# Turning x1 to rows by DMA instead of by TensorE, and an order for two early subtractions

## The reference

```
h  = RMSNorm(x, g_mix)
qa,ka,va,qb,kb,vb,ga,gb = split(h @ w_in)
ya = block-sparse causal attention, 8 heads;  yb = sliding-window attention, 8 query and 2 key heads
merged = sigmoid(ga + b) * (ya @ w_branch_a) + sigmoid(gb + b) * (yb @ w_branch_b)
x1  = x + merged @ w_out
out = x1 + square(relu(RMSNorm(x1, g_ffn) @ w_ff1)) @ w_ff2
```

## Time and profile before

| What | Value |
|---|---|
| median of 3 runs | 674.53 us (673.7 to 674.6) |
| the profiled execution's own time | 676.32 us |
| its span, first to last instruction | 674.5 us |
| TensorE busy | 667.3 us |
| VectorE busy | 504.3 us |
| ScalarE busy | 370.9 us |
| GpSimd busy | 323.7 us |
| transposes of x1 (32 matmuls, L1686) | 272 ns each |

### The profile page before, as it was taken

The page is one execution under the profiler, slowest core; times in us unless marked ns, Lnnn a source line. Parts: engine busy times, 40 slices in busy tenths (PEclk is TensorE's granted clock), DMA queues, the critical chain, the costliest instruction groups (busy, mean ns, idle before and its releaser), DMA issues.

```text
span 674.5 us, 9477 instructions
## 1 busy us (share of the span) xinstructions
PE 667.3 (99%) x3238; PEld 552.9 (82%) x3238; DVE 504.3 (75%) x701; ACT 370.9 (55%) x662; POOL 323.7 (48%) x197
## 2 busy tenths in 40 slices
PE   8999999999999999999999999999999999999997
PEld 7788888888888888888888888888888888888886
DVE  5767998655555555875559879787897888879797
ACT  6567676776666566534357546253553615546360
POOL 1246676466555662444445536246453444436432
PEclk9999999999999999999999999999999999999999
DMA  8322242223323113554222322315132151330303
GB/s 308 106 95 93 73 130 83 80 79 95 94 94 94 64 47 116 166 184 174 89 70 93 130 88 86 131 62 182 54 106 94 62 187 62 96 120 3 125 0 125
DMA packets 22909, 69.87 MB, mean 104 GB/s; under 512 B 2731, under 2 KB 4011, under 8 KB 22876
## 3 DMA queue, kind: packets, MB, share of 16 engines
q1 hardware_dynamic: 22588, 68.92, 30.8%
q10 hardware_dynamic: 288, 0.52, 0.2%
HBM read 67.27 MB, written 2.16 MB: 103 GB/s over the span
## 4 chain that ended last, share of the span: by engine, by line
PE 95%; DMA 1%; SPq 1%; ACT 1%; DVE 1%; issue 0%; DVEq 0%
PE bank L1396 21%; PE bank L1398 21%; PE bank L1397 21%; PE bank L1714 8%; PE bank L1716 8%; PE bank L1717 8%; PE bank L1563 3%; PE bank L1547 2%; PE bank L1584 1%; PE bank L1586 1%; DMA w_raw<-slabs 1%; SPq L449 1%; ACT store L665 1%; PE bank L1686 1%; PE bank L1424 0%; PE bank L1425 0%
## 5 line engine op out<-in xcount | busy, mean ns | idle before, releaser
L543 POOL TENSOR_TENSOR w_lo<-w_raw,w_hi 128x1024 fp32r<-128x1024 f32 x77 | 190.3, 2476 | 234.7 <-ACT w_hi L637 228.9
L1396 PE MATMUL bank<-qk_hi,w_hi 128*128 128x512 f32 x320 | 125.0, 391 | 0.0
L1398 PE MATMUL bank<-qk_hi,w_lo 128*128 128x512 f32 x320 | 124.5, 389 | 0.0
L1397 PE MATMUL bank<-qk_lo,w_hi 128*128 128x512 f32 x320 | 124.5, 389 | 0.0
L1396 PE MATMUL bank<-x_hi,w_hi 128*128 128x512 f32 x304 | 122.1, 402 | 0.0
L1398 PE MATMUL bank<-x_hi,w_lo 128*128 128x512 f32 x304 | 118.8, 391 | 0.0
L1397 PE MATMUL bank<-x_lo,w_hi 128*128 128x512 f32 x304 | 118.4, 389 | 0.0
L637 ACT ACTIVATE w_hi<-w_raw 128x1024 fp32r<-128x1024 f32 x80 | 83.9, 1057 | 55.9 <-PE bank L1398 52.7
L1279 DVE SCALAR_TENSOR_TENSOR store<-bank,softmax,store 128x512 f32<-128x512 f32 x101 | 71.9, 744 | 22.9 <-PE bank L1717 22.8
L1714 PE MATMUL bank<-v_parts,x_hi 128*128 128x512 f32 (+1 forms) x218 | 84.5, 387 | 0.3 <-issue 0.3
L1717 PE MATMUL bank<-v_parts,x_lo 128*128 128x512 f32 (+1 forms) x218 | 84.4, 387 | 0.0
(11 more groups left out here) (167 smaller groups left out, 1213.1 us busy)
## 6 DMA issues: line engine op xcount, KB each, us to landing
w_raw<-slabs SPq DMA_DIRECT2D x80, 512.0 KB, 3.3
bias_m<-slabs SPq DMA_DIRECT2D x16, 512.0 KB, 3.4
qk_hi_again<-slabs SPq DMA_DIRECT2D x16, 512.0 KB, 4.9
store<-x_t SPq DMA_DIRECT2D x16, 256.0 KB, 3.5
bias_m<-tab_dram SPq DMA_DIRECT2D x8, 256.0 KB, 4.2
out<-store SPq DMA_DIRECT2D x7, 256.0 KB, 2.5
bias_m<-tab_dram SPq DMA_DIRECT2D x8, 128.0 KB, 3.5
w_raw<-slabs ACTq DMA_DIRECT2D x2, 256.0 KB, 3.7
```

Source lines behind the costliest of these rows:

```text
L543: pool.tensor_tensor(w_lo[:, g % WS, :], w_raw[:, g % RAW, :], w_hi[:, g % WS, :].bitcast(F32), ALU.subtract).then_inc(w_lo_ready, 1)
L1396: pe.matmul(out_, wh, xh, start=first, stop=False)
L1397: pe.matmul(out_, wh, xl, start=False, stop=False)
L1398: last = pe.matmul(out_, wl, xh, start=False, stop=end)
```

## The change

The transposes of x1 leave TensorE. ScalarE copies tile n, as it stands in SBUF, into two planes of 16-bit numbers (the lower and the upper half of each float32), and issues one DMA that transposes both planes at once: 128x1024 16-bit numbers, 256 KB. GpSimd joins the turned halves into `x1_rows`, one tile after each of the low parts of slabs G_OUT+3 to G_FF+2. Planes and turned planes are rings of two. The final row copy on ScalarE in chunk 0 is gone, and its signal for the product buffers moves to the first part of the last w_out slab. At the start GpSimd waits for `x_sum_lo` before the low part of slab 4. The reserve of SBUF for DMA descriptors is smaller, which makes room for the planes.

```
-            def x1_rows_copy(n):            # ScalarE
-                act.wait_ge(x1t_done, n + 1)
-                act.activation(x1_rows[:, :, P * n:P * n + P], bank[n % 5]...,
-                               ACT.Copy).then_inc(x1_rows_ready, 1)
+            def x1_planes(n):
+                if n >= 2:
+                    act.wait_ge(planes_turned[n % 2], 16 * (n // 2))
+                of = store[:, n, :].bitcast(U16).rearrange("p (n h) -> p h n", h=2)
+                for h in range(2):
+                    act.activation(planes[n % 2][:, h, :], of[:, h, :], ACT.Copy).then_inc(planes_ready, 1)
+            def x1_turn(n):
+                act.wait_ge(planes_ready, 2 * n + 2)
+                if n >= 2:
+                    act.wait_ge(x1_rows_ready, n - 1)
+                act.dma_start_transpose(plane_rows[n % 2][...].rearrange("p h t n -> p (h t) n"),
+                                        planes[n % 2][...].rearrange("p h n -> p (h n)")).then_inc(
+                                            planes_turned[n % 2], 16)
             for n in range(N_OUT):
                 split_hi(G_OUT + n + 2)
                 act.wait_ge(acc_read, read(G_OUT + n))
                 act.activation(qk_hi[:, n, :], store[:, n, :], ...)
-                if n:
-                    x1_rows_copy(n - 1)
+                x1_planes(n)
+                x1_turn(n)
...
             square(0, 0)
-            x1_rows_copy(KT - 1)
             chunk(0, first=True)
```

```
             pool.wait_ge(w_lo_ready, 3)      # GpSimd
+            pool.wait_ge(xsum_lo_ready, 1)
             for s in range(4, G_GATE + 2):
...
+            def x1_rows_join(n):
+                pool.wait_ge(planes_turned[n % 2], 16 * (n // 2 + 1))
+                to = x1_rows[:, :, P * n:P * n + P].bitcast(U16).rearrange("p t (n h) -> p h t n", h=2)
+                for h in range(2):
+                    last = pool.tensor_copy(to[:, h, :, :], plane_rows[n % 2][:, h, :, :])
+                last.then_inc(x1_rows_ready, 1)
             for g in range(LATE + 2, G_FF + 3):
                 split_lo(g, g + 3)
+                if g >= G_OUT + 3:
+                    x1_rows_join(g - G_OUT - 3)
```

```
-            x1_transpose(0)                  # TensorE
             for n in range(2, N_OUT):
                 out_part(n, range(KT))
-                x1_transpose(n - 1)
...
             last.then_inc(slab_done, 1)      # the first w_ff1 slab
-            x1_transpose(N_OUT - 1)
```

More of the change, by code:

```diff
@@ L92, in build @@
 def build(nc, x_t, slabs, params, table, onehot, tab_dram, out):
-    F32, R = mybir.dt.float32, mybir.dt.float32r
+    F32, R, U16 = mybir.dt.float32, mybir.dt.float32r, mybir.dt.uint16
     ALU, ACT = mybir.AluOpType, mybir.ActivationFunctionType
@@ L136, in build @@
         par = sb("par", [P, N_PAR], F32)
+        planes = [sb(f"planes{i}", [P, 2, S], U16) for i in range(2)]
+        plane_rows = [sb(f"plane_rows{i}", [P, 2, QT, P], U16) for i in range(2)]
         softmax = sb("softmax", [P, 3, 8], F32)
@@ L250, in build @@
         x1_hi_ready, x1_lo_ready = sem("x1_hi_ready"), sem("x1_lo_ready")
-        x1t_done, x1_rows_ready = sem("x1t_done"), sem("x1_rows_ready")
+        planes_ready, x1_rows_ready = sem("planes_ready"), sem("x1_rows_ready")
+        planes_turned = [sem("planes_turned0"), sem("planes_turned1")]
         ms2_ready, r2_ready = sem("ms2_ready"), sem("r2_ready")
@@ L812, in _ @@
                 act.activation(x_hi[:, n, :], tmp_a, ACT.Copy).then_inc(m_hi_ready, 1)
-            def x1_rows_copy(n):
-                act.wait_ge(x1t_done, n + 1)
-                act.activation(x1_rows[:, :, P * n:P * n + P], bank[n % 5][:, :].rearrange("p (t n) -> p t n", t=QT),
-                               ACT.Copy).then_inc(x1_rows_ready, 1)
+            def x1_planes(n):
[8 more added lines that the diff above has]
+                    act.wait_ge(x1_rows_ready, n - 1)
+                act.dma_start_transpose(plane_rows[n % 2][:, :, :, :].rearrange("p h t n -> p (h t) n"),
+                                        planes[n % 2][:, :, :].rearrange("p h n -> p (h n)")).then_inc(
+                                            planes_turned[n % 2], 16)
             for n in range(N_OUT):
@@ L1676, in out_part @@
                     last = slab_part(g, bank[5 + n % 2], from_x, [kt], kt == 0, kt == KT - 1)
+                    if (n, kt) == (N_OUT - 1, 0):
+                        last.then_inc(product_done, 2 * PRODUCTS)
                 if kts[-1] == KT - 1:
                     last.then_inc(slab_done, 1)
[L1680 to L1689, removed]
             out_part(0, range(KT - 1))
@@ L1694, in _ @@
             out_part(1, range(2, KT))
-            x1_transpose(0)
             for n in range(2, N_OUT):
                 out_part(n, range(KT))
-                x1_transpose(n - 1)
             def up(j, c):
@@ L1833 @@
     arrays = {k: np.ascontiguousarray(v) for k, v in arrays.items()}
-    nc = bacc.Bacc("TRN2", target_bir_lowering=False, num_devices=1)
+    nc = bacc.Bacc("TRN2", target_bir_lowering=False, num_devices=1, dynamic_dma_scratch_size=2048)
     F32 = mybir.dt.float32
```

## The result

The changed kernel takes 675.75 us (median of 16 runs, 675.18 to 676.64), the kernel before 674.42 (16 runs beside it, 672.88 to 676.55): ratio 1.0018, 95% interval 1.0011 to 1.0026. That is 1.2 to 1.3 us slower, just inside the bound of 0.2%; the forecast was 672.5.

The account below looks back on a forecast made before the run. TensorE, busy 667.3 of 674.5 us, was taken as the bound. Transposes -3.8, early wait -1.5 and stall at up(3) +3.3 gave -2.0 us off the 674.53 median: 672.5, range 669.3 to 679.5.

Parts of the forecast that it names:

- the 3.8 us of the transposes: TensorE's w_out stage: removing 32 transposes, eight groups of 0.475 us each, takes 3.8 us off the path.
- what was called hidden: w_out stage: ScalarE's DMA issue (1.5 us), the DMA's landing (5) and seven of eight GpSimd joins cost nothing.
- C: ScalarE in the w_out stage: the transposing issue holds its queue over 2.6 us; at 4 us, 680.7; chance 0.14.
- D: DMA in the w_out stage: turns slower than slabs, at 8 us each +12, 686.5; chance 0.07.
- the place and the mechanism of the new wait: up(3), third w_ff1 tile behind the first: TensorE waits for GpSimd's low part, GpSimd and VectorE alternating; 3.3 us.
- first step: Kernel start: with GpSimd waiting, x_sum_lo ends before TensorE asks for it; 1.5 us gained.
- Rival F: Kernel start: VectorE is slow by itself, so the early wait gives 1.5 less gain, 674.0; chance 0.05.
- second step: GpSimd behind the last w_out slab: the eighth join makes TensorE late at up(3), taken 3.3 us between 2.2 and 4.9.
- The list's last case: GpSimd's schedule before up(3) if joins queue behind VectorE turns: low part ends at 15.7, 4.9 us late.
- third step: TensorE's granted clock behind the stall at up(3): the forecast's sum had no term for a fall.
- rival E: up(3): full 4.9 us stall and the clock falls, 3 us more, 677.1; chance 0.06 with the fall, 0.12 without.
- the 1.8 us around the span: Whole kernel: profiled execution took 676.32 with span 674.5; this remainder was assumed untouched by the change.

Follow-up runs that it names:

- e10: The kernel before, unchanged, profiled a second time: 672.90 us (1 run), span 671.1.
- e3: The changed kernel with the eighth join on ScalarE instead of GpSimd: 669.63 us, ratio 0.9942 to the kernel before.
- e11: The changed kernel with the eighth join on ScalarE and without the early wait: 669.62 us, ratio 0.9929 to the kernel before.
- e1: The kernel before with the early wait alone (GpSimd's low part of slab 4 behind x_sum_lo): 673.63 us, ratio 0.9997.
- e9: The kernel before with VectorE's x_sum_lo forced to wait for GpSimd's low part of slab 4: 675.70 us, ratio 1.0029.
- e2: The changed kernel without the early wait: 676.11 us, ratio 1.0037 to the kernel before.
- e6: The changed kernel with one copy instead of two in the eighth join: 673.61 us, ratio 0.999 to the kernel before.
- e5: The kernel before with the transposes of x1 left out and x1 not turned, no early wait, DMA or join: 670.18 us, ratio 0.9949.
- e4: The changed kernel with GpSimd making the low part of G_FF+3 before down_lo(0) in the first chunk: 670.72 us, ratio 0.9958 to before.
- e8: The changed kernel with the eighth join on ScalarE and the low part of G_FF+3 ahead of down_lo(0): 670.68 us, ratio 0.9957 to before.

## Why the prediction was wrong

**Right: the 3.8 us of the transposes.** Slabs are 5.44 apart, and e10 and e3, two profiles without collision or stall, are 671.1 - 667.6 = 3.5 us apart in span (e11: 671.1 - 667.2 = 3.9). (5.92 - 5.44 is 0.48 and not 0.475; the sum moves by 0.04.)

**Right: what was called hidden.** The issue took 1.25 us (taken 1.5, harmless up to 2.6), the landing 5.0 (taken 5), and seven of the eight joins cost TensorE nothing. Rivals C and D fall with these two numbers. For the issue, the Trainium skill ("DMA: Bandwidth & Descriptors", the cycles for each transpose instruction) gave an estimated 1.7; the trace has 1.25. For the turn, its 1309 ns for one 128x128 turn ("VectorE: DVE Perf Modes", the three transpose paths), multiplied by eight, gave an estimated 10.5; the trace has 5.0 for all eight in one DMA, so that figure is not to be multiplied.

**Right: the place and the mechanism of the new wait**, up(3)'s third tile behind the first, from GpSimd and VectorE taking turns.

**Wrong, first step: "Gain 27.51 - 26.01 = 1.5 us ... Taken: 1.5."** Measured: 0.0 between the medians of e11 and e3, and a ratio of 0.9997 in e1, 0.2 us. The price of one collision was right (e9); that a median holds it was not. The step read a collision from the earlier trace rows in which GpSimd was ahead by 24.61 - 24.53 = 0.08 us. In e10 and e2 VectorE is ahead, GpSimd begins within 0.02 us of x_sum_lo's end, and the delay is not there. The warning stood in the numbers that the sum itself used: the profiled execution took 676.32, 1.8 above the median. It was late at the start of slab 4 by 30.61 - 28.42 = 2.2 us against e10 (whose PE row is at 28.42), the collision among it. A gain that only such an execution has cannot be subtracted from a median. Rival F, which gave 674.0 by this step alone, was right in the size of this step for a wrong reason: VectorE was not slow by itself.

**Wrong, second step: "Between 2.2 and 4.9 I take 3.3: the joins queue, but not each time."** They queue each time: the one copy of e6 takes 1.77 us in place of 0.76, and the one that it leaves out gives 1.63 back. The list's last case put the low part's end at T8 + 15.7 (4.8 late against 10.9, not 4.9); it came at 357.97 - 343.06 = 14.9, and up(3) 4.15 late. The details err both ways: joins and down_lo(0) together took 354.67 - 347.98 = 6.7, not 8.1 (turns overlap the copies in part, though a copy takes 0.76 and not 0.65), and the low part itself met VectorE as well and took 3.3, not 2.4. By the Trainium skill ("SBUF — State Buffer", the reading of its port diagram) a GpSimd operation that reads SBUF and a two-input VectorE one exclude one another; the rows of e6 agree for a one-input copy. Compromise between two mechanisms was the mistake: either copies queue or they do not, and 3.3 was a number that neither gives.

**Wrong, third step: the clock.** The forecast had none of it; only rival E did, at 3 us, with a chance of 0.06. Over the span it was 0.997 or 0.995 in all 16 runs, and 0.999 or 1.0 in every run of the kernel before in the three sets of the experiments. It cost 2.7 us in the profiled run and, by an estimate, 2.0 in those at 0.997: their lowest span is 673.3, e3's and e11's 667.2, and 4.15 of the 6.1 between them is the stall. Rival E's "some 3 us of stream would take 6" had no row behind it; the trace has 2.95 in 5.68. The evidence in the earlier trace rows was one idle of 1.33 us without a fall, and it says nothing of one of 4.

**The sum with measured terms**: -3.8 + 0 + 4.15 + 2.0 to 2.7 = +2.35 to +3.05 us, on the lowest spans of before, 671.0 to 671.5, gives 673.4 to 674.6, which is where the changed kernel's are. But before's own spans go from 670.9 to 674.9: of the 47 in the three sets here 17 lie at or below 671.5, and the medians at 672.3 to 672.8. Against such a median +2.35 to +3.05 becomes +0.6 to +2.3, around the measured +1.3, which is also why rival E's 677.1 was 1.3 too high. Where the upper spans come from stays open. Of the 3.4 us between the two profiles of before, 0.6 lie ahead of the mean square, where the weight loads take a median of 7.5 us to land against 6.5, about 1.5 are the collision, 0.7 are two late starts among TensorE's last products (654.04 and 660.04), and 0.35 lie behind the last matmul. It is not the early collision alone, since e1, with the wait, goes from 670.9 to 673.7; and e3, e5 and e11, without TensorE's transposes and without the long stall, keep within 0.6 us each.

Two smaller premises of the sum failed as well. "The runs of this kernel lie within 0.9 us of each other" was read from three runs; the 16 lie 3.7 us apart. And the 1.8 us around the span did not stay: they are 1.9 to 2.0 in the changed kernel and 2.1 to 2.3 in e3 and e11, for a reason that no run shows.

## What to carry to other kernels

When an item is put into an engine's queue, look at what stands behind it until the queue next runs dry, and price the item as its own time and, where the other engine of a pair that takes turns is busy, one turn of that engine for each instruction put in: here 0.76 us of copy became 1.77 (e6). The first iteration behind the stage was where that queue had no slack, and another engine in the old place of the work (e3) was worth more than a better order (e4, e8). A row that hangs on a tie of under 0.1 us in one execution is not a term: hold the execution's own time against the median first. And price a long stall of TensorE twice, once for itself and once for the clock: behind the 4.0 us here the clock took 2.0 to 2.7 more in every run, with a stall of some 2.4 us about 1.5 in 7 of 11 (e6).

## What the runs showed of the hardware

- The granted clock over the span was 0.997 or less in all 16 runs of the changed kernel and all 6 of e2 (TensorE idle for 4.0 us in the profiled ones), in 7 of 11 runs of e6 (idle 2.37 in the profiled one, which is not among the seven), and in none of the 11 of e3 and e11. In the trace it went to its 1.2 GHz level during the 4.0 us, and thirteen matmuls took 5.68 us, some 0.43 each, before it came back.
- One DMA that turns a 128x1024 tile of 16-bit halves, from SBUF to SBUF, holds ScalarE's queue for 1.25 us and lands in 5.0.
- A GpSimd copy of 128x512 16-bit elements takes 0.76 us alone, and 1.77 with VectorE's two-input operations beside it. ScalarE makes two copies of that size in 1.13 us out of a float32 tile and in 1.42 into one.
